# Memory output, norm and router done token tile by token tile, and routing with fp32r parts

## The chip, the cores and the metric

The kernel runs on one NeuronCore of a Trainium2 chip. The metric is the device time of one execution in microseconds. It runs on five engines: TensorE (PE in the profile), VectorE (DVE), ScalarE (ACT), GpSimd (POOL) and SyncE (SP), which here only issues DMAs.

## The reference

One encoder layer over 512 tokens of width 1024 in fp32: a Hyena mixer and a grouped-query attention, an output projection with a residual, a cross attention to 256 memory rows, and a mixture of 16 experts. The part that matters here:

```python
x = x + memory_cross_attn(...)            # ends in  o @ w_o : 512x512 by 512x1024
h = rms_norm(x, norm_moe)
grp_prob = softmax(h @ w_rg + b_rg)       # 4 groups, take the best one
sel = (h @ w_re + b_re)[best group]       # 4 experts in it
w_top, e_loc = top_k(softmax(sel), 2)     # two experts per token
w_top = p_grp * w_top / sum(w_top)
for e in range(16):
    a = silu(h @ w_gate[e]) * (h @ w_up[e])
    y = y + gates[:, e:e+1] * (a @ w_down[e])
x = x + y
```

## The kernel before

The 512 tokens are four tiles of 128. A matmul with fp32 accuracy is made in three fp32r matmuls: each operand is split into a high part (a copy with rounding, by ScalarE) and a low part (a subtraction, by VectorE), and high by high, high by low and low by high are summed in PSUM. The weights ahead of the experts come in 42 pieces of 512 KB through a ring of three slots (`w_raw`, `w_hi`, `w_lo`), loaded by SP in `load_piece`, split by `weight_hi` (L635) and `weight_lo` (L995). Piece 41 is the last quarter of the memory output weights and could be loaded only when piece 38 had been used.

Every engine has one instruction list, written by hand in order, and semaphores tie them. PSUM has eight banks which a list of jobs (`psum_jobs`) hands out in turn; a job opens its bank when the earlier one is freed. There is no planner: the order in each engine's block is the order of the work.

Around the change the order is this. Memory attention runs in eight steps: scores, a maximum, an exponential (ScalarE), a normalisation (VectorE), transposes. Its output is split (`mo`, L640 and L1001). `chunk_jobs` (matmuls at L1698) multiplies by the output weights, piece by piece, each piece over all four token tiles, first the left 512 columns of all tiles and then the right. VectorE adds the residual into `x2` (L1348). Then all of `x2` is transposed (L1650), the transposes are scaled by `norm_moe` and copied to `hT` by both engines (L873, L1407), and only then the router runs for all four tiles, in fp32 (L1643; one fp32 matmul is two records in the trace). ScalarE squares the rows for the norm (L822), VectorE makes `xn` (L1425), and GpSimd stores `xn` to HBM, for the gather.

Routing is a chain of small VectorE instructions (`link` makes each wait for the one before): choice of the group and of two experts as one-hot rows (L1436 to L1462), gate weights (L1466 to L1472), one-hots over 16 experts (L1478, L1481), a count by two fp32 matmuls against a triangular and an all-ones matrix (L1932, L1933), running sums, the place of each token within its expert's block for all 64 columns, then one-hots of places and blocks (L1544 to L1548), an fp32 matmul which turns them into a table of token numbers and gates by block (`records`), and the table of experts (`e_tab`). The table of records is fp32. GpSimd casts a column of it to an int32 index (L532) and gathers 128 rows of `xn` (L536).

An expert block is gathered, transposed (`rows_T`, L1953), split (L899, L1588), multiplied (`gate_up`, `down`, L1958 to L1960), and added into the output by a scatter. Expert weights come in slots of 2 MB, six of them (three kinds, two sets). ScalarE splits them in quarters (L886), VectorE makes the low parts (L1576). The first turn is written out, the rest is a loop over two blocks.

## Time and profile before

| What | us |
|---|---|
| Median of 3 runs | 849.27 (847.8 to 849.71) |
| The profiled execution's own time | 847.16 |
| Its span | 845.3 |
| Output matmuls of the memory attention begin | 473.10 |
| First expert matmul | 544.68 |

| Engine | busy us | share of the span |
|---|---|---|
| PE | 758.9 | 90% |
| PEld | 610.2 | 72% |
| DVE | 595.4 | 70% |
| ACT | 453.8 | 54% |
| POOL | 78.0 | 9% |

PE is the matmul part of TensorE, PEld its weight load, which overlaps PE. Busy time of PE is modelled and counts pipelined matmuls in full. Times in a timeline are from the span's start. The granted clock is the part of 2.4 GHz that TensorE got: 1.00 or 0.50. The span lies inside the execution's own time.

### The profile page before, as it was taken

The numbers are of one execution on the slowest core, as the hardware profiler recorded it, in microseconds if no ns is written. First come the engines' busy times: TensorE is split into PE (matmuls) and PEld (weight loads), VectorE is DVE, ScalarE is ACT, GpSimd is POOL, SyncE is SP. The second block draws the span as 40 slices with busy tenths as digits, with TensorE's granted clock in tenths as the row PEclk, the third lists the DMA queues.
The fourth block names the chain that finished last, engine by engine and source line by source line (L and its number), as shares of the span: only waits on it lengthen the run. The fifth ranks groups of instructions, "written<-read, shape, count | busy, mean of one in ns | idle before, by whom it ended". The sixth has DMA issues, their size and how long they took to land.

```text
span 845.3 us, 10692 instructions
## 1 busy us (share of the span) xinstructions
PE 758.9 (90%) x3632; PEld 610.2 (72%) x3632; DVE 595.4 (70%) x897; ACT 453.8 (54%) x666; POOL 78.0 (9%) x92
## 2 busy tenths in 40 slices
PE   5699999988988899999896992499999999999994
PEld 3564867675777899978774682478888888888883
DVE  5368453994799688633537238578899998999892
ACT  6653323121234766521448151177888878888773
POOL 0000000000000000000000002202232222323101
PEclk9899999999989999979999985599999999999998
DMA  8620303120120200012230059869999999999941
GB/s 286 265 86 16 83 19 98 28 73 1 51 74 26 100 1 2 1 50 74 75 100 1 26 203 344 318 250 359 369 384 366 372 379 382 387 371 373 341 180 20
DMA packets 28542, 146.51 MB, mean 173 GB/s; under 512 B 4792, under 2 KB 6712, under 8 KB 21977
## 3 DMA queue, kind: packets, MB, share of 16 engines
q1 hardware_dynamic: 23320, 135.53, 43.1%
q0 software_dynamic: 5184, 10.50, 4.7%
q8 instruction: 22, 0.36, 0.2%
q14 instruction: 16, 0.12, 0.0%
HBM read 141.81 MB, written 12.58 MB: 183 GB/s over the span
## 4 chain that ended last, share of the span: by engine, by line
PE 76%; DVE 10%; DMA 6%; ACT 5%; issue 2%; SPq 1%; POOL 0%; POOLq 0%; DVEq 0%; ACTq 0%
PE bank L1698 20%; PE bank L1643 18%; PE bank L1958 10%; PE bank L1960 10%; PE bank L1959 10%; PE bank L1650 4%; PE bank L1953 2%; DMA slot<-in_w_down 2%; PE bank L1710 2%; DMA x_in<-in_x 1%; DMA w_raw<-in_w_in 1%; ACT junk L596 1%; ACT w_hi L635 1%; DVE w_lo L995 1%; PE bank L1982 1%
## 5 line engine op out<-in xcount | busy, mean ns | idle before, releaser
L1576 DVE TENSOR_TENSOR e_lo<-slot,e_hi 128x1024 fp32r<-128x1024 f32 x192 | 222.0, 1220 | 14.4 <-ACT e_hi L886 14.3
L886 ACT ACTIVATE e_hi<-slot 128x1024 fp32r<-128x1024 f32 x192 | 188.6, 1061 | 14.3 <-DMA slot<-in_w_down 6.2
L995 DVE TENSOR_TENSOR w_lo<-w_raw,w_hi 128x1024 fp32r<-128x1024 f32 x42 | 50.7, 1223 | 93.0 <-ACT w_hi L635 92.8
L635 ACT ACTIVATE w_hi<-w_raw 128x1024 fp32r<-128x1024 f32 x42 | 43.9, 1062 | 119.1 <-DMA w_raw<-in_w_in 65.9
L1958 PE MATMUL bank<-e_hi,hgT_hi 128*128 128x512 f32 x256 | 102.3, 400 | 3.7 <-DVE hgT_lo L1588 3.7
L1960 PE MATMUL bank<-e_hi,hgT_lo 128*128 128x512 f32 x256 | 100.6, 393 | 0.0
L1959 PE MATMUL bank<-e_lo,hgT_hi 128*128 128x512 f32 x256 | 100.6, 393 | 0.0
L1958 PEld LDWEIGHTS bank<-e_hi,hgT_hi 128*128 128x128 f32 x256 | 48.8, 191 | 13.9 <-DVE hgT_lo L1588 4.3
L1960 PEld LDWEIGHTS bank<-e_hi,hgT_lo 128*128 128x128 f32 x256 | 48.6, 190 | 10.5
L1959 PEld LDWEIGHTS bank<-e_lo,hgT_hi 128*128 128x128 f32 x256 | 48.7, 190 | 9.7
L1958 PE MATMUL bank<-e_hi,gaT_hi 128*128 128x512 f32 x120 | 48.1, 400 | 0.0
L899 ACT ACTIVATE hgT_hi<-bank 128x512 fp32r<-128x512 f32 x32 | 17.3, 595 | 55.3 <-PE bank L1953 55.3
L1960 PE MATMUL bank<-e_hi,gaT_lo 128*128 128x512 f32 x120 | 46.9, 391 | 0.0
L1959 PE MATMUL bank<-e_lo,gaT_hi 128*128 128x512 f32 x120 | 46.8, 390 | 0.0
L1698 PE MATMUL bank<-w_hi,hT_hi 128*128 128x512 f32 (+1 forms) x96 | 35.8, 373 | 4.7 <-DVE w_lo L995 3.2
L1698 PE MATMUL bank<-hT_hi,w_hi 128*128 128x512 f32 x96 | 38.3, 399 | 0.0
L1698 PE MATMUL bank<-hT_lo,w_hi 128*128 128x512 f32 x96 | 37.4, 389 | 0.0
L1698 PE MATMUL bank<-hT_hi,w_lo 128*128 128x512 f32 x96 | 37.4, 389 | 0.0
L1643 PE MATMUL bank<-v_hi,pT_lo 128*128 128x64 f32 x128 | 36.0, 282 | 0.0
L1643 PE MATMUL bank<-v_lo,pT_hi 128*128 128x64 f32 x128 | 35.9, 281 | 0.0
L1643 PE MATMUL bank<-v_hi,pT_hi 128*128 128x64 f32 x128 | 35.9, 281 | 0.0
L1698 PE MATMUL bank<-w_lo,hT_hi 128*128 128x512 f32 (+1 forms) x96 | 35.1, 366 | 0.0
(330 smaller groups left out, 1628.9 us busy)
## 6 DMA issues: line engine op xcount, KB each, us to landing
slot<-in_w_gate SPq DMA_DIRECT2D x16, 2048.0 KB
slot<-in_w_up SPq DMA_DIRECT2D x16, 2048.0 KB, 16.7
slot<-in_w_down SPq DMA_DIRECT2D x16, 2048.0 KB, 15.8
w_raw<-in_w_in SPq DMA_DIRECT2D x18, 512.0 KB, 3.6
w_raw<-in_w_out SPq DMA_DIRECT2D x8, 512.0 KB, 3.7
w_raw<-in_w_k_mem SPq DMA_DIRECT2D x4, 512.0 KB, 6.2
x_in<-in_x SPq DMA_DIRECT2D x4, 512.0 KB, 9.1
w_raw<-in_w_v_mem SPq DMA_DIRECT2D x4, 512.0 KB, 5.4
```

The costliest lines, as they stand in the source:

```text
L635: act.activation(w_hi[m % NSLOT][:], w_raw[m % NSLOT][:], ACT.Copy).then_inc(s_wh, 1)
L886: act.activation(e_hi[buffer(b, j)][:], slot[slot_][:, 1024 * part:1024 * (part + 1)], ACT.Copy).then_inc(s_ehi, 1)
L899: ins = act.activation(hgT_hi[:, 512 * half:512 * (half + 1)], banks[half][:], ACT.Copy)
L995: dve.tensor_tensor(w_lo[slot_][:], w_raw[slot_][:], w_hi[slot_][:].bitcast(F32), ALU.subtract)\
L1576: dve.tensor_tensor(e_lo[slot_][:, at_], slot[slot_][:, at_], e_hi[buffer(b, j)][:].bitcast(F32), ALU.subtract)\
L1643: ins = pe.matmul(dst, l, r, start=(n == 0), stop=(n == len(pairs) - 1))
L1650: ins = pe.transpose(bank(job)[:, n * width:(n + 1) * width], s, ident[:])
L1698: ins = pe.matmul(bank(job)[:, 0:width], left, right, start=(k == 0 and m == 0), stop=(final and m == 2))
L1710: done(pe.matmul(bank(job)[:], a2[:, t * P:(t + 1) * P], w3[way][:, o, :], start=True, stop=True))
L1958: pe.matmul(dst, act_hi, w_hi_, start=first, stop=False)
L1959: pe.matmul(dst, act_hi, w_lo_, start=False, stop=False)
L1960: return pe.matmul(dst, act_lo, w_hi_, start=False, stop=last)
```

## The change

1. The memory output is computed by token tile: both halves of tiles 0 and 1, transposes of tile 0, both halves of tile 2, router of tile 0, transposes of tile 1, and so on (`wom_tile`, `x2T_jobs`, `router_job`). Residual, squares, norm, `xn` and its store follow tile by tile.
2. The last weight piece has a fourth ring slot at 24 KB. It is loaded without waiting for a slot and split inside the memory attention loop.
3. The router multiplies unscaled `x2`, in a high and a low part, with router weights that VectorE scales by `norm_moe` and splits (`wr_split`, 40 columns: high and low). All its matmuls are fp32r. The norm's factor is applied to the logits.
4. The counts are fp32r matmuls that also sum over the tiles. Places and blocks are chosen per token (8 values) and not for all 64 columns. The prefix over experts is a masked sum (`less`) in place of four shift steps.
5. The one-hots of places are eight instructions, each with a semaphore, and the record matmuls follow them one by one. The token number is a record of its own (`rec_i`, int32 at once); gates go through a second matmul later (`rhs_g`, `gates`, `rec_g`).
6. GpSimd's first four gathers read `rec_i` directly. The clearing of the gather buffers goes. The gate records and the expert table are finished after the first rows are split (`tables`).
7. The first block's rows are split by halves with a semaphore for each (`first_rows_hi`, `first_rows_lo`); the matmuls wait for the second half only at the third weight piece.
8. SP loads expert slots 2 and 5 first, slots 0 and 1 after the last tile of the output, 3 and 4 after the last router and all `xn` stores. `xn` moves to 136 KB, so that slot 5 is free.

```diff
-    jobs += [("hT", 2, k) for k in range(KT)]
-    jobs += [("router",), ("count",), ("records",)]
+    jobs += [("wom", 0, 0), ("wom", 1, 0), ("wom", 0, 1), ("wom", 1, 1), ("x2T", 0, 0), ("x2T", 0, 1)]
+    jobs += [("wom", 0, 2), ("wom", 1, 2), ("router", 0), ("x2T", 1, 0), ("x2T", 1, 1)]
+    jobs += [("wom", 0, 3), ("router", 1), ("x2T", 2, 0), ("x2T", 2, 1), ("wom", 1, 3)]
+    jobs += [("router", 2), ("x2T", 3, 0), ("x2T", 3, 1), ("router", 3)]
+    jobs += [("count",), ("records",), ("gates",)]
...
-                sp_.dma_start(slot_view(s), views[s][:, 0]).then_inc(w_ld[s], 16)
+            sp_.dma_start(slot_view(2), views[2][:, 0]).then_inc(w_ld[2], 16)
+            sp_.dma_start(slot_view(5), views[2][:, 1]).then_inc(w_ld[5], 16)
             for i in range(TT):
                 wait_freed(sp_, ("wom", 1, i))
+                if i == TT - 1:
+                    for s in range(2):
+                        sp_.dma_start(slot_view(s), views[s][:, 0]).then_inc(w_ld[s], 16)
                 sp_.dma_start(out[0, i * P:(i + 1) * P, :], x2[:, i, :]).then_inc(s_base, 16)
-            wait_freed(sp_, ("router",))
+            wait_freed(sp_, ("router", TT - 1))
             sp_.wait_ge(s_store, 16 * TT)
             for s in range(3, 5):
                 sp_.dma_start(slot_view(s), views[s - 3][:, 1]).then_inc(w_ld[s], 16)
-            sp_.wait_ge(s_gath[1], 16)
-            sp_.dma_start(slot_view(5), views[2][:, 1]).then_inc(w_ld[5], 16)
             sp_.wait_ge(s_tab, 1)
             nb = sp_.value_load(e_tab[0:1, 31:32], min_val=0, max_val=MAXB - NE) + NE
 
...
 
             def meta(b, q):
 
                 if not isinstance(b, int) or b >= 2:
                     pool.wait_ge(s_oa, b - 1)
...
-                if not isinstance(b, int) or b >= 2:
+                if isinstance(b, int):
+                    index = rec_i[:, b:b + 1]
+                    if b >= 2:
+                        pool.wait_ge(s_t, 2 * b - 2)
+                else:
+                    index = gather_i[:, q, :]
                     pool.wait_ge(s_t, 2 * b - 2)
...
+                if s == 2:
+                    weight_hi(final_piece, 1)
...
+            def x2T_hi(i):
+                for h in range(2):
+                    job = ("x2T", i, h)
+                    wait_filled(act, job)
+                    act.activation(hT_hi[:, 4 * h:4 * h + 4, i * P:(i + 1) * P], bank(job)[:].rearrange("p (k n) -> p k n", k=4),
+                                   ACT.Copy).then_inc(s_hi, 1)
+
+            tile_norm(12, "wom", 10, 0)
+            x2T_hi(0)
+            tile_norm(12, "wom", 10, 1)
+            x2T_hi(1)
...
+            def first_rows_hi():
+                for half, sem_ in ((0, s_first_hi), (1, s_rhi)):
+                    act.wait_ge(s_t, half + 1)
+                    act.activation(hgT_hi[:, 512 * half:512 * (half + 1)], banks[half][:], ACT.Copy).then_inc(sem_, 1)
...
+                if s == 3:
+                    weight_lo(final_piece, 1)
...
+            def x2T_lo(i):
+                for h in range(2):
+                    job = ("x2T", i, h)
+                    dve.wait_ge(s_hi, splits.index(job) + 1)
+                    at_ = (slice(None), slice(4 * h, 4 * h + 4), slice(i * P, (i + 1) * P))
+                    free(dve.tensor_tensor(hT_lo[at_], bank(job)[:].rearrange("p (k n) -> p k n", k=4), hT_hi[at_].bitcast(F32),
+                                           ALU.subtract), job)
+
+            def tile_xn(i):
+                dve.wait_ge(s_rms, 2 + TT + i + 1)
+                link(dve.reciprocal(small[:, 28 + i:29 + i], small[:, 28 + i:29 + i]))
                 dve.scalar_tensor_tensor(xn[:, i, :], x2[:, i, :], small[:, 28 + i:29 + i], g_moe[:], ALU.mult, ALU.mult)\
                     .then_inc(s_xn, 1)
...
+            def tile_logits(i):
+                job, r = ("router", i), small[:, 28 + i:29 + i]
+                wait_filled(dve, job)
+                part_ = rt[:, 2720 + 20 * i:2740 + 20 * i]
+                link(dve.scalar_tensor_tensor(part_, bank(job)[:, 20:40], r, row("b_router"), ALU.mult, ALU.add))
+                free(dve.scalar_tensor_tensor(lg[:, i, :], bank(job)[:, 0:20], r, part_, ALU.mult, ALU.add), job)
...
+            link(dve.tensor_tensor(scaled, wr[:], cols[:, c0:c0 + KT].unsqueeze(2).to_broadcast([P, KT, NG + NE]), ALU.mult))
+            link(dve.tensor_copy(wr_split[:, :, 0:20], scaled))
+            dve.tensor_tensor(wr_split[:, :, 20:40], scaled, wr_split[:, :, 0:20].bitcast(F32), ALU.subtract).then_inc(s_wr, 1)
...
+            dve.wait_ge(ld["g_moe"], 16)
+
+            tile_residual(0, 0)
+            tile_residual(0, 1)
+            tile_residual(1, 0)
+            tile_xn(0)
+            tile_residual(1, 1)
+            x2T_lo(0)
+            tile_residual(2, 0)
+            tile_xn(1)
+            tile_residual(2, 1)
+            x2T_lo(1)
+            tile_residual(3, 0)
+            tile_xn(2)
+            x2T_lo(2)
+            tile_logits(0)
+            tile_logits(1)
+            tile_residual(3, 1)
+            x2T_lo(3)
+            tile_xn(3)
+            tile_logits(2)
+            tile_logits(3)
+            wait_freed(dve, ("router", TT - 1))
...
+            both4 = R3(2816, 4)
+            link(dve.tensor_tensor(both4, oh1, oh2, ALU.add))
+            E12 = onehots[:].rearrange("p (t g e) -> p t g e", t=TT, g=NG)
+            for t in range(TT):
+                dve.tensor_tensor(E12[:, t], ohg[:, t, :].unsqueeze(2).to_broadcast([P, NG, EPG]),
+                                  both4[:, t, :].unsqueeze(1).to_broadcast([P, NG, EPG]), ALU.mult).then_inc(s_oh, 1)
...
+            job = ("count",)
+            wait_filled(dve, job)
+            pos, cnt = bank(job)[:, 0:64], bank(job)[:, 64:80]
+            ov, exc, shift = R(720, 16), R(736, 16), R(752, 16)
+            above(ov, cnt, (128, 256, 384), ALU.is_gt)
+            prefix = rt[:, 1380:1636].rearrange("p (a b) -> p a b", a=NE)
+            link(dve.tensor_tensor(prefix, less[:], ov.unsqueeze(1).to_broadcast([P, NE, NE]), ALU.mult))
+            at_place = R(1100, 128)
+            dve.tensor_tensor(at_place.rearrange("p (r n) -> p r n", r=2), both.rearrange("p (r t) e -> p r (t e)", r=2),
+                              pos.unsqueeze(1).to_broadcast([P, 2, 64]), ALU.mult)
+            link(dve.tensor_reduce(exc, prefix, AX.X, ALU.add))
+            psel = R(1240, 8)
+            dve.tensor_reduce(psel, at_place.rearrange("p (g e) -> p g e", e=NE), AX.X, ALU.add)
+            link(dve.tensor_tensor(shift, exc, x_const, ALU.add))
+            moved = R(1250, 128).rearrange("p (g e) -> p g e", e=NE)
+            hi, xsel, places, blocks = R(780, 8), R(800, 8), R(820, 8), R(840, 8)
+            dve.tensor_tensor(moved, both, shift.unsqueeze(1).to_broadcast([P, 2 * TT, NE]), ALU.mult)
+            link(dve.tensor_scalar(hi, psel, 128.0, None, ALU.is_ge))
+            dve.tensor_reduce(xsel, moved, AX.X, ALU.add)
+            link(dve.scalar_tensor_tensor(hi, psel, 256.0, hi, ALU.is_ge, ALU.add))
+            link(dve.scalar_tensor_tensor(hi, psel, 384.0, hi, ALU.is_ge, ALU.add))
+            dve.scalar_tensor_tensor(places, hi, -128.0, psel, ALU.mult, ALU.add)
+            link(dve.tensor_tensor(R(860, 8), hi, xsel, ALU.add))
+            dve.tensor_tensor(vals, vals, places, ALU.subtract)
+            link(dve.scalar_tensor_tensor(blocks, hi, 0.0, R(860, 8), ALU.is_gt, ALU.mult))
+            link(dve.tensor_tensor(blocks, blocks, chosen, ALU.add))
+            free(dve.tensor_tensor(R(880, 16), exc, ov, ALU.add), job)
+            wait_freed(dve, job)
+            inc = R(880, 16)
+            for g in range(2 * TT):
+                dve.tensor_scalar(place_oh[:, g, :], iota[:], places[:, g:g + 1], None, ALU.is_equal)
+                dve.tensor_scalar(rhs_i[:, g, :], iota[:, 0:MAXB], blocks[:, g:g + 1], vals[:, g:g + 1], ALU.is_equal, ALU.mult)\
+                    .then_inc(s_slot, 1)
+
...
             link(dve.tensor_scalar(R(264, 4), R(204, 4), 1.0, None, ALU.add))
             link(dve.reciprocal(R(264, 4), R(264, 4)))
+            job = ("records",)
+            wait_filled(dve, job)
+            free(dve.tensor_scalar(rec_i[:, 0:MAXB], bank(job)[:, 0:MAXB], col("spare"), None, ALU.add), job)
+            wait_freed(dve, job)
+            dve.sem_inc(s_rec, 1)
...
+            gates, gates_lo = R(268, 8), R(2840, 8)
+            link(dve.tensor_copy(gates_hi[:], gates))
+            link(dve.tensor_tensor(gates_lo, gates, gates_hi[:].bitcast(F32), ALU.subtract))
+            for g in range(2 * TT):
+                dve.tensor_scalar(rhs_g[:, g, 0, :], iota[:, 0:MAXB], blocks[:, g:g + 1], gates_hi[:, g:g + 1].bitcast(F32),
+                                  ALU.is_equal, ALU.mult)
+                dve.tensor_scalar(rhs_g[:, g, 1, :], iota[:, 0:MAXB], blocks[:, g:g + 1], gates_lo[:, g:g + 1],
+                                  ALU.is_equal, ALU.mult).then_inc(s_grhs, 1)
+
+            def tables():
+                job = ("gates",)
+                wait_filled(dve, job)
+                link(dve.tensor_copy(rec_g[:, 0:MAXB], bank(job)[:, 0:MAXB]))
+                free(dve.tensor_tensor(rec_g[:, 0:MAXB], rec_g[:, 0:MAXB], bank(job)[:, MAXB:2 * MAXB], ALU.add), job)
+                wait_freed(dve, job)
+                dve.sem_inc(s_recg, 1)
...
                 act_mul(b)
                 rows_lo(b + 1)
 
-            dve.wait_ge(s_tab, 1)
             turn(0, 0)
...
+            def wom_tile(i, h):
+                job = ("wom", h, i)
+                open_bank(pe, job)
+                n0 = first_piece[f"wom{h}"]
+                for n in (n0, n0 + 1):
+                    pe.wait_ge(s_wl, n + 1)
+                    wh, wl = piece_view(w_hi, n), piece_view(w_lo, n)
+                    for kk in range(2):
+                        k = 2 * (n - n0) + kk
+                        if i == 0 and h == 0:
+                            wait_freed(pe, ("mo", k))
+                        tile_ = slice(i * P, (i + 1) * P)
+                        pe.matmul(bank(job)[:], moT_hi[:, k, tile_], wh[:, kk, :], start=(k == 0), stop=False)
+                        pe.matmul(bank(job)[:], moT_hi[:, k, tile_], wl[:, kk, :], start=False, stop=False)
+                        ins = pe.matmul(bank(job)[:], moT_lo[:, k, tile_], wh[:, kk, :], start=False, stop=(k == MH - 1))
+                done(ins)
...
+            def router_job(i):
+                job = ("router", i)
+                open_bank(pe, job)
+                tile_ = slice(i * P, (i + 1) * P)
+                for h in range(2):
+                    wait_freed(pe, ("x2T", i, h))
+                    for k in range(4 * h, 4 * h + 4):
+                        pe.matmul(bank(job)[:, 0:40], hT_hi[:, k, tile_], wr_split[:, k, :], start=(k == 0), stop=False)
+                        ins = pe.matmul(bank(job)[:, 0:40], hT_lo[:, k, tile_], wr_split[:, k, :], start=False, stop=(k == KT - 1))
+                done(ins)
...
+            x2T_jobs(0)
+            wom_tile(2, 0)
+            wom_tile(2, 1)
+            pe.wait_ge(s_wr, 1)
+            router_job(0)
+            x2T_jobs(1)
+            wom_tile(3, 0)
+            router_job(1)
+            x2T_jobs(2)
+            wom_tile(3, 1)
+            router_job(2)
+            x2T_jobs(3)
+            router_job(3)
...
+            pe.wait_ge(s_oh, TT)
+            pe.matmul(bank(job)[:, 0:64], tri_r[:], onehots[:], start=True, stop=False)
+            for t in range(1, TT):
+                pe.matmul(bank(job)[:, NE * t:64], ones_r[:], onehots[:, 0:64 - NE * t], start=False, stop=(t == TT - 1))
+            done(accumulate(job, bank(job)[:, 64:64 + NE], [(ones_r[:], onehots[:, NE * t:NE * (t + 1)]) for t in range(TT)]))
...
+            for g in range(2 * TT):
+                pe.wait_ge(s_slot, g + 1)
+                ins = pe.matmul(bank(job)[:, 0:MAXB], place_oh[:, g, :], rhs_i[:, g, :], start=(g == 0), stop=(g == 2 * TT - 1))
+            done(ins)
+            job = ("gates",)
+            open_bank(pe, job)
+            pe.wait_ge(s_grhs, 2 * TT)
...
+                else:
+                    pe.wait_ge(s_rlo, b + 1)
...
                 for j in range(8):
                     kind, part = j // 4, j % 4
...
```

## Rows read from the trace of the kernel before

**Rows 1.** the chain of waits, 440 to 600 us; columns: start, us, what

```profile
473.10 21.81 PE bank L1698 x96
...
494.91 3.51 PE bank L1650 x32
...
499.56 11.95 PE bank L1643 x64
...
529.63 3.63 PE bank L1643 x16
...
533.53 0.26 DVE rec_sb L1569
...
535.91 4.20 DMA hg<-xn_dram,gather_i
...
540.24 1.96 PE bank L1953 x8
...
543.34 1.30 DVE hgT_lo L1588 x2
...
544.68 0.80 PE bank L1958
```

**Rows 2.** three stretches: busy time by engine, PE clock, DMA share, GB/s

```profile
300.00:320.00 20.00, 20.00 (x163) 18.79 (x163) 17.00 (x33) 11.77 (x26) 0.00 (x0) 1.00 0.00 1
...
501.80:549.50 47.70, 21.16 (x86) 19.37 (x86) 31.03 (x111) 13.06 (x21) 9.45 (x16) 0.50 0.87 341
...
690.00:710.00 20.00, 20.00 (x95) 16.76 (x94) 18.54 (x19) 16.93 (x22) 5.98 (x6) 1.00 1.00 396
```

**Rows 3.** memory attention loop: ScalarE busy, PE clock, DMA share, GB/s

```profile
451.00:463.50 12.50, 12.49 (x39) 1.00 0.00 1
```

**Rows 4.** timelines of ScalarE and VectorE, the splits of the last weight piece

```profile
482.35 1.06 ACT L635 ACTIVATE w_hi<-w_raw 128x1024 fp32r<-128x1024 f32 x1 [8.61 <-DMA w_raw<-in_w_o_mem]
...
483.44 1.23 DVE L995 TENSOR_TENSOR w_lo<-w_raw,w_hi 128x1024 fp32r<-128x1024 f32 x1 [8.98 <-ACT w_hi L635]
```

**Rows 5.** timeline of TensorE, attention, first and last of twelve matmuls

```profile
298.85 0.28 PE L1643 MATMUL bank<-v_hi,pT_hi 128*128 128x64 f32 x1
...
300.08 0.28 PE L1643 MATMUL bank<-v_hi,pT_lo 128*128 128x64 f32 x1
```

**Rows 6.** timelines of ScalarE and VectorE, operations on halves and tiles

```profile
473.14 0.60 ACT L640 ACTIVATE moT_hi<-bank 128x512 fp32r<-128x512 f32 x1 [1.12 <-PE bank L1643]
...
501.25 1.04 ACT L822 ACTIVATE junk<-x 128x1024 f32<-128x1024 f32 x1
...
473.77 0.69 DVE L1001 SCALAR_TENSOR_TENSOR moT_lo<-bank,moT_hi 128x512 fp32r<-128x512 f32 x1 [1.03 <-ACT moT_hi L640]
...
484.59 2.48 DVE L1348 TENSOR_TENSOR x<-x,bank 128x512 f32<-128x512 f32 x4
...
505.68 4.87 DVE L1425 SCALAR_TENSOR_TENSOR xn<-x,small,g_moe 128x1024 f32<-128x1024 f32 x4
```

**Rows 7.** timeline of VectorE, routing and the first expert pieces

```profile
512.24 0.17 DVE L1436 TENSOR_REDUCE rt<-rt 128x4 f32<-128x16 f32 x1
...
516.24 0.18 DVE L1445 TENSOR_TENSOR rt<-rt 128x16 f32<-128x16 f32 x1
...
518.48 0.22 DVE L1481 TENSOR_TENSOR rt<-rt 128x64 f32<-128x64 f32 x1
...
533.69 4.63 DVE L1576 TENSOR_TENSOR e_lo<-slot,e_hi 128x1024 fp32r<-128x1024 f32 x4
```

**Rows 8.** timeline of GpSimd, the index cast

```profile
533.92 1.03 POOL L532 CAST gather_i<-rec_sb 128x1 int32<-128x1 f32 x1 [20.69 <-DVE rec_sb L1569]
```

**Rows 9.** DMA issues in three short windows; last column us to landing

```profile
xn_dram<-xn POOLq DMA_DIRECT2D x1, 512.0 KB, 15.0
...
g_moe<-in_g_moe SPq DMA_DIRECT2D x1, 512.0 KB, 3.8
...
slot<-in_w_up SPq DMA_DIRECT2D x1, 2048.0 KB, 12.3
```

313 lines of the change are left out of this document (135 added, 178 removed).

## The prediction

> **What bounds the kernel now.** I read the chain of waits first, then the granted clock by stretch, then the timelines of the four engines between 440 and 560 us, last the expert stage. The reader is to see three things.
>
> First, the expert stage (from 544.68 us to the end) is a convoy of TensorE. In [rows 2] the stretch 690 to 710 has PE busy for all 20 us at clock 1.00, with the DMA engines at 1.00 too. TensorE does not wait there, so whatever makes the stage begin earlier moves the whole stage, with its tail, by that much; its weight loads are released by TensorE's own progress and move with it. Second, everything between the memory output and the first expert matmul is one chain [rows 1]: 96 output matmuls from 473.10, 32 transposes, 64 router matmul records from 499.56, small VectorE instructions, the record matmuls at 529.63, the gather at 535.91, transposes at 540.24, the low halves at 543.34, and the expert matmuls at 544.68. That is 71.6 us with one engine at a time. Third, TensorE runs at half clock (granted 0.50, 1.2 of 2.4 GHz) from 501.8 to 549.5 [rows 2]: it fell behind the dense output matmuls, under transposes and 20-column matmuls.
>
> I cost the change against this chain, in four steps, in the time of the profiled execution (span 845.3, its own time 847.16), and carry the difference to the median of 849.27, which lies 2.1 above it.
>
> **Step A, the last weight piece (+2.4).** Piece 41 gets a slot of its own, loads right behind piece 40, and its split moves from 482.35 (ScalarE 1.06) and 483.44 (VectorE 1.23), where both engines idled, into the memory attention loop [rows 4]. There ScalarE is busy 12.49 of 12.5 us [rows 3], so its 1.06 less 0.1 of overlap goes straight onto the path: +1.0. VectorE must then wait for that split before its own 1.23, with the loop's next maximum and normalisation queued behind; the two engines hand to each other each step, so I count another 0.9. The load of piece 40 is waited for by ScalarE and now has piece 41 0.4 us behind it: +0.5. Bounds: 0.5 (all absorbed) to 4. The output matmuls begin at 475.5 instead of 473.1. Call that t0.
>
> **Step B, output, residual, norm, router by tile (-4.6).** Before: 473.1 to 512.24, when VectorE starts routing [rows 7]: 39.1 us. After, TensorE's own work: 96 output matmuls 21.8 (21.81 for 96 [rows 1], 0.227 each, unchanged); transposes 8 per tile at 0.11, 0.9 per tile; router 16 fp32r matmuls of 40 columns per tile. No row has this shape. The nearest are the attention's 64-column fp32r matmuls, eleven steps from 298.85 to 300.08, 0.112 each at full clock [rows 5]; the bounds are half of that and, at half clock, 0.22 (the record matmuls: 3.63 for 16 [rows 1]). I take 0.112, 1.8 per tile. TensorE order: all eight output groups, three tiles of transposes (2.6) and two routers (3.6) end at t0+28.1. Then the third router and last transposes run to t0+30.8, while VectorE adds the last residual (0.62 [rows 6]) and ScalarE squares and roots it (1.04 for the square [rows 6], 1.5 in all by my estimate), so ScalarE is free at t0+30.4. High halves 0.60 and low halves 0.69 [rows 6] of the two half tiles overlap: all ready at t0+32.3, the last router matmuls end at t0+33.4. VectorE still has the last norm product (1.2 [rows 6]) and four small logit instructions: routing begins at t0+34.6 = 510.1. The residuals of the earlier tiles, their squares, halves and xn products (18 us of VectorE work) lie under 28 us of matmuls. VectorE starts them only when g_moe has landed, 3.8 after its issue [rows 9], at about t0+6; the first tile is needed by TensorE at t0+10.9, so this is covered with 3.5 to spare. Should the clock already be at half for the final router, +1.5.
>
> **Step C, routing (-6.8).** Before: 512.24 to 533.79 [rows 1, 7], 21.5 us. After, by VectorE's pace of one dependent small instruction per 0.2 us. Selection as before, 4.2 [rows 7], then one small sum and four products: one-hots at +4.9 instead of +6.5, because the gate arithmetic (six instructions) and half of the one-hots move behind. Count on TensorE: 8 fp32r matmuls in place of 4 records, at half clock 0.22 each: 2.2 with the hand-over. Places chosen per token: some 21 instructions, a good half of them dependent, two over 256 elements which I put at 0.45 (between 0.2 for 16 columns and 0.62 for 512 [rows 6]): 4.1. Eight place one-hots with their columns, at 0.25 a pair: 2.0, and TensorE's eight record matmuls follow behind each, in place of 3.63 after the last. Then VectorE has six gate instructions in its queue ahead of the record read: 1.25, which covers the last record matmul. The record read with its cast to int32: 0.3. Sum 4.9+2.2+4.1+2.0+1.25+0.3 = 14.75. Bounds: 12 (overlap inside the independent pairs) to 18. Records ready at 524.9.
>
> **Step D, gather to first expert matmul (-3.1).** Before: 533.79 to 544.68, 10.9 us. The cast on GpSimd (1.03 [rows 8]) and its own semaphore go: the gather is issued 0.5 after the record instead of 2.1. It lands after 4.2 [rows 1]; the first four transposes take 1.0 (1.96 for eight [rows 1]); the high and low half 0.60 and 0.69: 7.2. But VectorE, which in the old kernel split the first four expert pieces (4.63 [rows 7]) while the gather flew, now first has two gate products, a rounding, a subtraction and 16 small gate columns: 2.4, then 4.63, then the first low half 0.69: 7.8 with hand-over. VectorE ends last; 7.8 stands. Behind it the table work (2.7) sits before expert pieces 4 and 5; their first use is 24 matmuls later, 7.5 at half clock and 5.5 at full, and they are ready 4.5 after the start. So the tables cost nothing; without this cover they would cost up to 2.7.
>
> **The moved loads.** SP issues expert pieces 2 and 5 at about 477.5, behind g_moe, and 0 and 1 only at t0+28.8 = 504.3. A pair of 2 MB loads landed in 12.3 [rows 9]; ScalarE has them by 517, and VectorE wants them at 527.3. Pieces 3 and 4 still wait for the last router and for all xn stores. The last xn store is issued near 509.4; before, such a store took 15.0 to land [rows 9], with some 10 MB in flight; here 5 MB are. Even 15.0 gives 524.4, just under the records at 524.9, for which the gather waits as well. Pieces 3 and 4 then land by 537 and are wanted near 541. The cleared gather buffers (two memsets on GpSimd) were under the routing: nothing.
>
> **One rule weighed.** [Rows 7] and [rows 1] show the gather issued at 535.91 while VectorE ran two-input subtractions, and nothing slow in it. The Trainium skill, "SBUF — State Buffer", section "Who interferes with whom", says that one-source VectorE instructions (copy, cast, tensor_scalar) in a two-port mode keep GpSimd out of the shared port, so that it cannot write the descriptors of its own DMA. Here the gather is written just while VectorE runs the gate columns, which are such instructions. No run so far shows it; it is the fourth rival below.
>
> **Sum.** +2.4 - 4.6 - 6.8 - 3.1 = -12.1. Expert matmuls begin at 532.6. 847.16 - 12.1 = 835.1 for a profiled execution, 849.27 - 12.1 = 837.2 for the median.
>
> **The rivals.**
> 1. *The clock falls at the first router block* (t0+17.3) and stays at 1.2 GHz. Then 15.3 us of TensorE work (two output tiles with their transposes and routers) doubles: +15, 852, slower. It decides from 12.1 us of extra. For it: the clock fell just there in the old order, 7 us behind the last dense matmul [rows 2]. Against: dense 2.7 to 5.5 us groups stand between the small ones, and the attention, with 64-column matmuls, transposes and a few wide ones mixed, holds 1.00 [rows 2]. Chance 0.06. A partial form, from the third router on: +3.6, 840.8, chance 0.12.
> 2. *The last xn store holds the gather* and pieces 3 and 4: at a landing of 20 instead of at most 15, +4.5, 841.7. For it: 15.0 already stands within 0.5 of the path. Against: half the bytes in flight. 0.07.
> 3. *The tiles don't overlap*, because VectorE is held for g_moe: landing like a store (13 and more) it would delay the first residual to 490 and TensorE by 5: 842. Against: 3.8 in the same company before. 0.05.
> 4. *GpSimd's descriptors wait for VectorE's gate columns*: the gather is written 2.4 later, of which 0.6 is slack: +1.8, 839. 0.10.
>
> **How the numbers follow.** Forecast 0.60, with steps A to D at their own bounds 833 to 841. The range 831.5 to 843.5 takes in rivals 2 to 4 and the partial clock, and leaves out the full clock case and unforeseen waits. This kernel's measurement tells about 0.2% (1.7 us) from no change. Faster: 0.92; within: 0.02; slower 0.06.
>
> **What would show it.** A: output matmuls begin near 475.5, ScalarE's split of the last piece inside the loop. B: granted clock 1.00 up to about 505, routing begins near 510. C: records near 525, VectorE without gaps except one of about 0.6 before the count. D: gather issued within 0.5 of the record, first expert matmul near 532.6, its first low half last. Expert stage: TensorE without a gap as before, and as long. Wrong if the clock is at 0.50 by 495, if the first expert matmul comes after 542, or if the stage, once begun, runs longer than its 300 us.

## The result, and the profile after

The changed kernel takes 839.15 us (median of 4 runs, 834.61 to 841.46) against 849.49 in the same session: ratio 0.989 [0.985, 0.993]. Forecast: 837.2, range 831.5 to 843.5, faster with 0.92. Its profiled execution takes 837.83 us (span 835.8) where 835.1 was forecast. The time was right to 2 us, partly by luck: an error in one step took off what an error in another had added (see the sum below).

The chain of waits after; it answers to [rows 1]:

```profile
474.36 0.23 PE bank L2025
...
502.17 0.24 PE bank L2027
...
506.10 0.26 PE bank L2042
...
510.05 0.18 DVE rt L1531
...
525.14 0.25 DVE rec_i L1626
...
529.66 4.54 DVE e_lo L1665 x4
...
534.19 0.61 DVE hgT_lo L1677
...
534.85 0.80 PE bank L2099
```

The first output matmul is at 474.36 (473.10 before), routing begins at 510.05 (512.24), the record is ready at 525.38 (533.79), the first expert matmul starts at 534.85 (544.68). The gather no longer stands in this chain: VectorE's low halves of the expert weights end last. The stage behind it is as long as before (300.95 us to the end, 300.62 before), so in these two profiles it moved as a whole. The windows, as in [rows 2] (columns: busy us by engine, TensorE clock, DMA share, GB/s):

```profile
501.80:506.30 4.50, 3.43 (x29) 3.15 (x28) 1.93 (x4) 3.03 (x6) 0.00 (x0) 1.00 0.49 132
506.30:547.00 40.70, 23.92 (x90) 20.33 (x90) 34.32 (x130) 15.21 (x19) 4.26 (x8) 0.58 0.67 261
690.00:710.00 20.00, 20.00 (x95) 16.74 (x95) 18.54 (x20) 16.94 (x22) 5.16 (x7) 1.00 1.01 384
```

The clock is at its higher level until the last tile's router and falls inside it. ScalarE, VectorE and TensorE in the memory loop, where [rows 4] had nothing (timelines: start, us, instruction, idle before it and its releaser):

```profile
459.04 1.06 ACT L662 ACTIVATE w_hi_last<-w_raw_last 128x1024 fp32r<-128x1024 f32 x1
...
460.13 1.22 DVE L1040 TENSOR_TENSOR w_lo_last<-w_raw_last,w_hi_last 128x1024 fp32r<-128x1024 f32 x1 [0.74 <-ACT w_hi_last L662]
...
462.14 0.66 PE L1746 MATMUL bank<-ident,pr 128*128 128x128 f32 x4 [1.97 <-DVE pr L1434]
...
467.26 7.11 PE L1739 MATMUL bank<-mpT,mv 128*128 128x512 f32 x16 [1.10 <-ACT mpT L886]
```

VectorE waits 0.74 for ScalarE's split, then spends 1.22 on its own, and TensorE idles 1.97 ahead of its fifth group of transposes. In the kernel before it had no gap there and one of 1.05 a step later:

```profile
460.69 0.66 PE L1650 MATMUL bank<-ident,pr 128*128 128x128 f32 x4
...
462.40 0.66 PE L1650 MATMUL bank<-ident,pr 128*128 128x128 f32 x4 [1.05 <-DVE pr L1389]
```

In the changed kernel that later gap is 0.87, so the two together cost 1.79 more. (The value matmuls, L1739 with `mpT` and `mv`, multiply the transposed probabilities by the memory's values; there are sixteen of 512 columns, and they end the loop.) VectorE in the routing; it answers to [rows 7]:

```profile
514.47 0.43 DVE L1564 TENSOR_TENSOR onehots<-rt 128x16 fp32r<-128x16 f32 x4
...
517.01 0.17 DVE L1580 TENSOR_SCALAR rt<-bank 128x16 f32<-128x16 f32 x1 [0.78 <-PE bank L1739]
...
521.12 0.29 DVE L1614 TENSOR_SCALAR place_oh<-iota,rt 128x128 fp32r<-128x128 f32 x1
521.33 0.29 DVE L1615 TENSOR_SCALAR rhs_i<-iota,rt 128x24 fp32r<-128x24 f32 x1
...
524.30 0.18 DVE L1619 TENSOR_REDUCE rt<-rt 128x4 f32<-128x16 f32 x1
...
525.14 0.24 DVE L1626 TENSOR_SCALAR rec_i<-bank,cols 128x24 int32<-128x24 f32 x1
...
526.33 0.30 DVE L1635 TENSOR_SCALAR rhs_g<-iota,rt,gates_hi 128x24 fp32r<-128x24 f32 x1
...
526.93 0.52 DVE L1637 TENSOR_SCALAR rhs_g<-iota,rt 128x24 fp32r<-128x24 f32 x1
...
529.55 4.64 DVE L1665 TENSOR_TENSOR e_lo<-slot,e_hi 128x1024 fp32r<-128x1024 f32 x4
```

The eight pairs take 3.2 us (0.2 for each instruction, 24 columns wide or 128). GpSimd's gather, where the cast of [rows 8] is gone, and the landings of the last xn store and of the gather, answering to [rows 9] (last column: us from issue):

```profile
526.38 1.09 POOL L562 DMA_INDIRECT hg<-xn_dram,rec_i  x1 [17.62 <-DVEq L1628]
```

```profile
xn_dram<-xn POOLq DMA_DIRECT2D x1, 512.0 KB, 9.6
...
hg<-xn_dram,rec_i POOLq DMA_INDIRECT x1, 5.1
```

### The profile page after: what moved, and what is told of

It reads as the page before. It is cut to its first block, busy times and chain, and to the rows that moved or that the text cites. A ratio compares the mean times of both kernels' runs of the same rounds, so it can differ in the third digit from the quotient of the medians.

```text
span 835.8 us, 10729 instructions
## 1 busy us (share of the span) xinstructions
PE 762.1 (91%) x3636; PEld 611.9 (73%) x3636; DVE 603.5 (72%) x937; ACT 456.4 (55%) x670; POOL 73.4 (9%) x86
## 4 chain that ended last, share of the span: by engine, by line
PE 76%; DVE 10%; DMA 6%; ACT 5%; issue 2%; SPq 1%; POOL 0%; DVEq 0%; POOLq 0%; ACTq 0%
PE bank L1794 18%; PE bank L1739 16%; PE bank L2099 10%; PE bank L2101 10%; PE bank L2100 10%; PE bank L1746 4%; DMA slot<-in_w_down 2%; PE bank L1806 2%; PE bank L2094 2%; DMA x_in<-in_x 1%; PE bank L2027 1%; PE bank L2026 1%; PE bank L2025 1%; DMA w_raw<-in_w_in 1%; ACT junk L623 1%
## 5 line engine op out<-in xcount | busy, mean ns | idle before, releaser
L1665 DVE TENSOR_TENSOR e_lo<-slot,e_hi 128x1024 fp32r<-128x1024 f32 x192 | 221.8, 1220 | 11.2 <-ACT e_hi L926 10.9
L662 ACT ACTIVATE w_hi<-w_raw 128x1024 fp32r<-128x1024 f32 x41 | 42.9, 1063 | 111.7 <-DMA w_raw<-in_w_in 66.6
L1739 PE MATMUL bank<-v_hi,pT_lo 128*128 128x64 f32 x128 | 35.5, 277 | 0.0
L1739 PE MATMUL bank<-v_lo,pT_hi 128*128 128x64 f32 x128 | 35.5, 277 | 0.0
L1739 PE MATMUL bank<-v_hi,pT_hi 128*128 128x64 f32 x128 | 35.5, 277 | 0.0
L1794 PE MATMUL bank<-w_lo,hT_hi 128*128 128x512 f32 (+1 forms) x96 | 34.5, 360 | 0.0
L1794 PE MATMUL bank<-w_hi,hT_lo 128*128 128x512 f32 (+1 forms) x96 | 34.5, 359 | 0.0
```

The lines of the kernel that those rows point to most:

```text
L662: act.activation(w_hi[ring(m)][:], w_raw[ring(m)][:], ACT.Copy).then_inc(s_wh, 1)
L1665: dve.tensor_tensor(e_lo[slot_][:, at_], slot[slot_][:, at_], e_hi[buffer(b, j)][:].bitcast(F32), ALU.subtract)\
L1739: ins = pe.matmul(dst, l, r, start=(n == 0), stop=(n == len(pairs) - 1))
L1794: ins = pe.matmul(bank(job)[:, 0:width], left, right, start=(k == 0 and m == 0), stop=(final and m == 2))
```

## The experiments

Twelve runs in three sessions. The kernel before had medians of 846.53, 846.75 and 848.11 us in them; the ratios are against it. They are the ratios on record and not quotients of two medians, from which they differ by up to 0.003 (for e8 0.9841 and 0.987). All were profiled, and their profiles put side by side, in us:

```
                          first loop      ->       ->       -> first   ->
                          transpose ->    routing  record   expert     end
                          output matmul   begins   ready    matmul
before                    18.50           39.70    21.54    10.90      300.62
split in loop alone       23.27           38.69    21.54    11.22      302.48
changed, first profile    20.27           36.25    15.33     9.47      300.95
changed, e0               23.86           35.12    15.32    10.26      298.88
changed, e12              22.77           35.98    15.30     9.45      301.87
e3 no interleave          23.30           36.61    15.30     9.46      300.28
e4 wide gates             23.25           35.32    15.30     9.92      302.18
e9 gap filled             20.26           35.78    15.30     9.49      300.72
e1 split behind loop      18.48           35.02    15.29    10.39      299.02
e8 the same again         20.18           35.65    15.33     9.62      301.83
e5 e1 + wide, gates late  20.19           35.62    14.49    10.64      299.43
e6 e5 + loads held        18.50           34.99    14.50     8.18      304.02
e10 e1 + routing filled   20.17           34.98    15.24    10.67      300.18
e11 e5 + routing filled   20.18           35.02    14.30    11.59      299.88
```

(The output matmul is taken where the timeline has its first record, 0.56 ahead of the chain's start for it.) Profiles are single executions. Columns two to four repeat within about 1 us for the same code. In column two the last tile's router begins 32.3 after the first output matmul in every version but e3 and the two old ones; what follows depends on where in it the clock falls (not at all in e1, e6, e10 and e11, with 35.0). The first column does not repeat, and the clock is why (below). So it is with the last: 301.8 to 304.0 in e4, e6, e7, e8 and e12, where the granted clock is 0.83 to 0.92 both over 10 to 20 and over 280 to 290 us behind the first expert matmul; 300.3 and 300.7 in e3 and e9, with the first of these dips alone; 298.9 to 300.95 in the others, with neither.

**e0_after**, the changed kernel itself, as the yardstick of the first session.

> The changed kernel again, as the reference of this chip and for its spread. My theory of the change: 10 us faster than before (about 839), with the same landmarks in the trace: output matmuls begin 1.3 to 2.5 us later than in the kernel before if both reach the memory attention together, routing takes 15.3, the way from the records to the first expert matmul 9.5. Rival for its spread (834.6 to 841.5 in four runs): stretches of half clock ahead of the changed part, in the attention, fall differently from run to run; then the time from the first transposes of the memory attention to the end agrees within 1 us between two profiles, while the time up to them differs by several.

Measured: 840.07 us (10 runs, 834.81 to 841.22), 0.9907 [0.9874, 0.9939]. This profile has what the first one did not: the clock falls in the memory loop. TensorE's timeline, and a window over it:

```profile
464.26 0.66 PE L1746 MATMUL bank<-ident,pr 128*128 128x128 f32 x4 [2.37 <-DVE pr L1434]
...
469.84 9.85 PE L1739 MATMUL bank<-mpT,mv 128*128 128x512 f32 x16 [1.10 <-ACT mpT L886]
```

```profile
466.00:470.00 4.00, 2.90 (x13) 2.12 (x13) 1.40 (x6) 2.44 (x7) 0.00 (x0) 0.50 0.00 0
```

The sixteen value matmuls take 9.85 instead of 7.11: the granted clock is 0.50 (1.2 GHz) from about 465.1 to 475.4 and 1.00 from there on. The gather ends last here: its flight is on the chain with 6.62 us, and the first expert matmul waits for it and not for VectorE's expert pieces:

```profile
530.56 6.62 DMA hg<-xn_dram,rec_i
```

The rival of the expectation, that only what lies ahead of the memory attention differs, fails: from the loop's first transposes to the end the changed kernel takes 382.3 (first profile), 383.4 (e0) and 385.4 us (e12), where it asked for agreement within 1.

**e1_split_in_gap and e8_split_in_gap_again**: step A undone in part. The last piece keeps its own slot and early load, but both halves are split just behind the loop:

```diff
-                if s == 2:
-                    weight_hi(final_piece, 1)
+            weight_hi(final_piece, 1)
             for h in range(MH):
                 split_hi(("mo", h), moT_hi[:, h, :])
...
-                if s == 3:
-                    weight_lo(final_piece, 1)
+            weight_lo(final_piece, 1)
             for h in range(MH):
                 split_lo(...)
```

> The split of the last weight piece moves from inside the memory attention loop to the gap behind it, where both engines wait for the mo matmuls. Theory (step A): in the loop it lies on the path, so from the first transposes of the loop to the first mo matmul 1.8 us go (13.7 becomes 12.0, as in the kernel before), and the kernel is 1.8 us faster than the changed one. Rival: the loop is held by TensorE and the other waits, and the split costs nothing there: 0, the 1.8 come from elsewhere. Second rival: behind the loop the split delays the halves of mo and the first output group: 0 or slower.

> The kernel of the second run once more (split behind the loop, all else changed), for its spread and a second profile, and as the reference of the next two. Theory: the clock stays at 1.00 from the loop through the mo matmuls, 18.5 us to the first output matmul, median near 834, 5 to 6 us faster than the changed kernel. Rival (luck): the fall is chance and comes here too: 20 to 23 us, median 838 to 840.

Measured: 833.97 (0.9857 [0.9812, 0.9902]) and 835.53 (0.9841 [0.9814, 0.9867]). Beside e0, in the same session, e1 is 6.1 us lower by the medians (831.4 to 838.1 against 834.8 to 841.2). By the ratios, which compare across sessions, the two are 0.003 to 0.007 below the changed kernel's 0.9889 to 0.9907, or 3 to 6 us. With e5 and e6 they are the fastest versions of this study. TensorE's timeline of e1:

```profile
459.75 0.66 PE L1744 MATMUL bank<-ident,pr 128*128 128x128 f32 x4 [1.05 <-DVE pr L1433]
...
463.34 7.11 PE L1737 MATMUL bank<-mpT,mv 128*128 128x512 f32 x16 [1.09 <-ACT mpT L886]
```

No gap of 2 us, loop and value matmuls as long as before. The two splits (1.05 and 1.23 here) lie where both engines wait for the value matmuls. In the profile of e8 the same code lost the clock all the same, but later, under the value matmuls, and for 3 to 4 us, which cost 1.7:

```profile
466.14 8.80 PE L1737 MATMUL bank<-mpT,mv 128*128 128x512 f32 x16 [1.10 <-ACT mpT L886]
```

**e7_before_split_in_loop**: step A alone. The kernel before, with the slot of its own for piece 41 and the splits at s == 2 and s == 3 of the loop, and nothing else of the change:

```diff
                     mem_exp(s + MAHEAD)
+                if s == 2:
+                    weight_hi(final_piece, 1)
...
                     mem_max(s + MAHEAD)
+                if s == 3:
+                    weight_lo(final_piece, 1)
```

> The kernel before with step A alone: own slot for the last weight piece, its split inside the memory attention loop; all else as before. Theory: the split holds both engines, TensorE stands idle for 2 us in the loop, and in most executions the clock then falls to 0.50, so that the last transposes and the mo matmuls run at half. From the loop's first transposes to the first output matmul 20.3 us where the clock holds and 23.3 to 23.9 where it falls, against 18.5 before; the kernel 2 to 5 us slower than before, and with a wider spread. Rival 1: the clock fell in three profiles because of what came earlier (the start of the loop at half clock), not because of the gap; then this one keeps 1.00 in the loop and is 1.8 slower. Rival 2: the delay belongs to the other changes; then within 0.2% of before.

Measured: 852.53 us (848.07 to 854.11) where before has 846.75: 1.005 [1.0025, 1.0074], so 4.2 us slower, 2.1 to 6.3 by the interval (5.8 by the medians). TensorE's timeline shows gap and fall again:

```profile
463.21 0.71 PE L1663 MATMUL bank<-ident,pr 128*128 128x128 f32 x4 [1.97 <-DVE pr L1401]
...
468.78 9.65 PE L1656 MATMUL bank<-mpT,mv 128*128 128x512 f32 x16 [1.10 <-ACT mpT L870]
```

**e9_gap_filled and e12_after_again**: is the gap what lowers the clock? Ten identity transposes on TensorE ahead of the wait at s == 4, in the bank that the real ones then overwrite, beside the changed kernel once more:

```diff
+            def fill(job, n):
+                open_bank(pe, job)
+                for _ in range(n):
+                    pe.transpose(bank(job)[:, 0:P], ident[:], ident[:])
...
+                if s == 4:
+                    fill(("MPT", s), 10)
                 pe.wait_ge(s_mnorm, s + 1)
```

> The changed kernel with ten more 128x128 transposes of the identity on TensorE in the memory loop, ahead of its wait for the fifth probability tile (the 2 us gap that the in-loop split of the last weight piece opens); they write the bank that the real transposes overwrite, and end before these may start (10 x 0.165 = 1.65 us of a gap of 1.97 to 2.37). Theory one: the gap is why the granted clock falls to 0.50 in the loop (4 of 5 profiles with the in-loop split), so with it filled the clock is 1.00 through the loop and the mo matmuls (x16) take 7.1 us and not 9.6 to 9.9; from the first loop transpose to the first output matmul 20.3 us as where the clock held, and the time falls by 2 to 3 us against the changed kernel (about 837.5 where it is 840). Theory two: the clock falls for other reasons (the loop's small matmuls altogether); then mo stays at 9.6 to 9.9 and the time is that of the changed kernel, or up to 1.5 us above it if ten transposes at the half clock (3.3 us) outlast the gap.

> The changed kernel once more, beside the three filled ones. By both theories 838 to 841 with the spread seen before (834.8 to 841.2); if the in-loop gap is what lowers the clock, this profile shows the mo matmuls at 9.6 to 9.9 us more likely than at 7.1 (four of five so far).

Measured: 838.9 (834.0 to 840.05), 0.9888 [0.9846, 0.993], beside 839.33 (837.44 to 843.82), 0.9897 [0.9857, 0.9937]. TensorE's timeline of e9:

```profile
461.32 1.26 PE L1745 MATMUL bank<-ident 128*128 128x128 f32 x10
463.45 0.66 PE L1751 MATMUL bank<-ident,pr 128*128 128x128 f32 x4 [0.87 <-DVE pr L1434]
...
468.56 7.11 PE L1739 MATMUL bank<-mpT,mv 128*128 128x512 f32 x16 [1.10 <-ACT mpT L886]
```

The profile is as the gap theory has it: the clock holds, the idle time is 0.87. It is one profile, and the first of the changed kernel held the clock without a filler. The times don't part the two (0.4 us, with intervals of 3.5 to either side), where the theory wanted 2 to 3 us. So: the gap's 1.8 us is shown; that it draws the clock down has five profiles of six with an unfilled gap for it (e0, e3, e4, e7, e12, not the first), and no time. The rival that the expectation of e7 names, that what came earlier decides, is not excluded. In all fourteen profiles the clock was at half some way ahead of the loop and was back 1 to 7 us before the loop's first transposes. By that alone they don't part: it was back 1.1 to 1.2 before in e3, e4 and e7, which fell 0.4 to 0.5 behind the gap, and 1.3 before in e9, which held. No run varied it.

**e3_no_interleave**: step B undone in its order, with the rest of the change kept. All output tiles, then all transposes, then all routers:

```diff
+            for i in range(TT):
+                wom_tile(i, 0)
+                wom_tile(i, 1)
+            for i in range(TT):
+                x2T_jobs(i)
+            pe.wait_ge(s_wr, 1)
+            for i in range(TT):
+                router_job(i)
```

(in place of the mixed order; ScalarE's and VectorE's calls follow it.)

> The new operations in the old order: all eight output groups, then all transposes, then all four routers; residual, norm and xn still by tile where the matmuls allow. Theory (step B): what the mixed order gains is that small matmuls stand between dense groups and the clock stays at 1.00 until the last tile. Then here the clock falls under the routers, some 7 us behind the last dense group, and routing begins 1 to 4 us later after the output matmuls begin than the changed kernel's 35.7. Rival (overlap): the gain is that norm, halves and residual lie under matmuls; then the last tile's work is exposed in one piece and it is 3 to 6 us later at an unchanged clock. Second rival: the order gives nothing, it is the merged scaling and norm that gained; then routing begins within 0.7 of 35.7.

Measured: 841.03, 0.9932 [0.9898, 0.9965], against 0.9907 for e0. These two runs are of one session, and their times are not told apart. From output to routing 36.61 us against 35.12 to 36.25 for the changed kernel. Here too the clock falls under the last routers, in a window that TensorE fills:

```profile
508.00:512.00 4.00, 4.00 (x21) 4.00 (x20) 2.25 (x7) 0.00 (x0) 0.53 (x1) 0.50 1.03 382
```

By these single profiles the order is worth 0.4 to 1.5 of step B's 3.5 us, where the changed kernel's own three differ by 1.1. The rest goes with what e3 keeps: residuals and norm by tile, and the router in fp32r parts (64 matmuls of 40 columns, where there were 64 records in 11.95 at half clock). Those two were not tried apart.

**e4_wide_gates**: the 16 gate columns as three wide products:

```diff
-            for g in range(2 * TT):
-                dve.tensor_scalar(rhs_g[:, g, 0, :], iota[:, 0:MAXB], ..., ALU.is_equal, ALU.mult)
-                dve.tensor_scalar(rhs_g[:, g, 1, :], ...)
+            dve.tensor_tensor(block_oh, iota..., blocks..., ALU.is_equal)
+            dve.tensor_tensor(rhs_g[:, :, 0, :], block_oh, gates_hi..., ALU.mult)
+            dve.tensor_tensor(rhs_g[:, :, 1, :], block_oh, gates_lo..., ALU.mult)
```

> The 16 small gate columns (3.3 us of VectorE between the records and the first expert pieces) become one block one-hot and two wide products (1.0). Theory (step D): VectorE ends last, but the gather is close behind: issued 1.0 after the records, landing 5.1, then 1.0 for four transposes, 0.6 and 0.7 for the halves, 8.5 in all, against 9.5 now. So the first expert matmul comes 1.0 us sooner after the records, and the kernel is 1.0 faster than the changed one. Rival 1: VectorE alone sets it: 2.3 sooner. Rival 2: the gate matmuls or the gather set it already: 0.

Measured: 838.28, 0.9893 [0.9845, 0.9941], not told apart from e0. VectorE's timeline:

```profile
527.41 0.35 DVE L1639 TENSOR_TENSOR rhs_g<-rt 128x192 fp32r<-128x192 f32 x1
527.68 4.62 DVE L1667 TENSOR_TENSOR e_lo<-slot,e_hi 128x1024 fp32r<-128x1024 f32 x4
535.07 0.69 DVE L1679 TENSOR_TENSOR hgT_lo<-bank,hgT_hi 128x512 fp32r<-128x512 f32 x1 [2.77 <-ACT hgT_hi L939]
```

VectorE starts on the expert pieces 1.8 after the record instead of 4.2 and then waits 2.77 for the gathered rows: its gain turned into a wait for the gather, which took 6.3 here.

**e5_all**: e1, the block one-hots of the records wide as well, and all gate work behind the first expert pieces:

```diff
-            for g in range(2 * TT):
-                dve.tensor_scalar(place_oh[:, g, :], ...)
-                dve.tensor_scalar(rhs_i[:, g, :], ...)
+            link(dve.tensor_tensor(block_oh, iota..., blocks..., ALU.is_equal))
+            link(dve.tensor_tensor(rhs_i[:], block_oh, vals..., ALU.mult))
+            for g in range(2 * TT):
+                dve.tensor_scalar(place_oh[:, g, :], ...).then_inc(s_slot, 1)
...
-                    lo_parts(b, q, 4, 8)
+                    lo_parts(b, q, 4, 7)
+                    gate_columns()
+                    lo_parts(b, q, 7, 8)
                     lo_parts(1, 1, 0, 4)
+                    gate_records()
```

> Split behind the loop; block one-hots and columns as wide products for the records and the gates; gate columns, gate matmuls and gate records only after the first block's expert pieces, beside its matmuls. Theory: records 0.9 sooner (16 small instructions become 8 and two wide ones); after them VectorE takes 4.6 for the expert pieces and the gather ends last, issued 1.0 after the records and landing 4.2 to 6.9: 8 to 10 us to the first expert matmul, so about 0 to 1 gained there. In all 1 to 2 us faster than the kernel with the split behind the loop. Rival 1: VectorE set the way to the first expert matmul: 9.5 becomes 6.5, 3 to 4 faster. Rival 2: late gates delay the second gather round and the first turn's product: 0 or slower.

Measured: 835.26, 0.9851 [0.9824, 0.9878]: no better than e8. The record comes 0.84 earlier (VectorE's timeline):

```profile
521.20 0.36 DVE L1612 TENSOR_TENSOR rt<-iota,rt 128x192 f32<-128x192 f32 x1
521.60 0.36 DVE L1614 TENSOR_TENSOR rhs_i<-rt 128x192 fp32r<-128x192 f32 x1
521.99 1.66 DVE L1616 TENSOR_SCALAR place_oh<-iota,rt 128x128 fp32r<-128x128 f32 x8
```

But the gather, issued earlier, flew 7.0 us on the chain, and the first expert matmul came 10.64 after the record.

**e6_loads_behind_gather**: e5 with slots 3 and 4 loaded only when the first gather has landed:

```diff
             sp_.wait_ge(s_store, 16 * TT)
+            sp_.wait_ge(s_gath[0], 16)
             for s in range(3, 5):
```

> The same with the loads of expert slots 3 and 4 held until the first gather has landed. Theory (the gather is slowed by 4 MB of weights in flight): the gather lands 2.9 to 3.5 after its issue in place of 4.2 to 6.9, the first expert matmul comes 7 to 7.5 after the records, 1.5 to 2.5 us better. But slots 3 and 4 land 12.3 after the gather, some 2 us before their first use by ScalarE. Rival 1: the landing is the gather's own latency (stores to HBM, 128 descriptors) and doesn't change: 0. Rival 2: the weights of the second block come late and TensorE waits in the second turn: slower by 2 to 4.

Measured: 834.43, 0.9844 [0.982, 0.9868]: e5's time. The chain shows the gather's flight at 4.54 us, beside no weight load, against e5's 7.0 (2.9 to 3.5 were expected):

```profile
519.80 4.54 DMA hg<-xn_dram,rec_i
```

The first expert matmul comes 8.18 after the record, 2.5 sooner than in e5, and the stage behind it is 4.6 longer. Windows of e6 and of e5, both from 20 to 30 us behind the first expert matmul:

```profile
546.98:556.98 10.00, 10.00 (x42) 8.18 (x41) 7.51 (x7) 6.74 (x7) 0.00 (x0) 0.91 0.74 277
```

```profile
555.27:565.27 10.00, 10.00 (x50) 8.42 (x49) 7.70 (x7) 6.59 (x8) 0.00 (x0) 1.00 0.78 281
```

TensorE is busy for all of both; e6 has the lower clock. Over the first three such stretches e6 has 0.76, 0.92 and 0.91 where e5 has 0.84, 1.00 and 1.00, which makes 2.5 us, and the transposes of the third block's rows are 2.4 later. The other 2.2 are lost behind the last rows' transposes, where e6 takes 42.9 to the end and e5 40.6; but e4, e8 and e12, whose loads are not held, take 42.3 to 42.6 there, so that part is not the loads' doing. Whether the held loads bring about the first is open: one profile, and a time that shows neither gain nor loss.

**e10_routing_filled and e11_all_filled**: e1 and e5 with idle TensorE fed in the routing by the same fill():

```diff
+            fill(("router", 3), 5)
             router_job(3)
             job = ("count",)
-            open_bank(pe, job)
+            fill(job, 16)
...
             job = ("records",)
-            open_bank(pe, job)
+            fill(job, 14)
```

(e10 also 14 ahead of the gates; e11 24 ahead of the gathered rows.)

> The split of the last weight piece behind the memory loop (e1), and idle TensorE fed with transposes of the identity in the routing: 5 ahead of the last tile's router matmuls (1.07 us idle), 16 ahead of the count (5.6 idle), 14 ahead of the records (4.9 idle), 14 ahead of the gates (5.0 idle); at half clock 16 last 5.3 us, so that they end about when the real work may begin. Theory one (activity holds the clock): the granted clock is above 0.50 in much of 508 to 536, the records matmuls take 1.5 instead of 3.08, the row transposes 1.0 instead of 1.9, the first expert matmuls run at the full clock; first expert matmul 1.5 to 3 us earlier and the expert stage up to 2 shorter: 831 to 832 where e1 is 835. Theory two (fillers of this size do not lift it, since they fill half of the time and the router and records matmuls stay small): the clock stays 0.50 and the time is e1's, up to 1.5 us above where a filler outlasts its gap.

> The version with the split behind the loop, the wide block one-hots and the gate columns behind the gather's issue (e5), with transposes of the identity on TensorE: 5 ahead of the last router, 16 ahead of the count, 14 ahead of the records and 24 ahead of the gathered rows' transposes (8.5 us idle). Theory one: the clock is 1.00 by the first expert matmul, which comes 1 us earlier, and the first two blocks lose less: about 832 where e5 is 835.3. Theory two: the clock stays at 0.50 until the expert matmuls have run for some us as in all profiles so far; 835, or up to 1.5 above.

Measured: 837.12, 0.986 [0.9816, 0.9903], and 837.25, 0.9876 [0.9835, 0.9917]: e1's time at best. Window and timeline of e10:

```profile
508.00:512.00 4.00, 1.64 (x16) 1.40 (x13) 3.45 (x23) 0.22 (x1) 0.53 (x1) 1.00 0.98 418
```

```profile
507.67 1.97 PE L1743 MATMUL bank<-ident 128*128 128x128 f32 x16
...
515.23 3.25 PE L1743 MATMUL bank<-ident 128*128 128x128 f32 x14
```

The clock holds through the last router and the first filler. Through the router it held in e1 and e6 as well, without fillers, and from output to routing these have the same 35.0; so that is not shown to be the fillers' doing. In e10 it is then at 0.50 for the second filler, comes up to 0.79 over 528 to 532 (the eight gate matmuls take 1.07 instead of 1.87), and is at 0.50 again for the gathered rows. At the first expert matmul it is at 0.50 in e10 and 0.53 in e11. The routing, VectorE's, gains 0.1. With these fillers TensorE still idles 1.7 to 4.1 us at all waits but one, and they don't bring the higher clock to where TensorE is the bound again.

## Why the prediction was right, and which steps were off

**Step A, predicted +2.4, is the step that failed.** Its mechanism (both splits on the path of a saturated hand-over, 1.0 + 0.9) is what the first profile shows, +1.77 inside the loop. The load's +0.5 lies ahead of the loop, where this column doesn't look: piece 40 was waited for 3.88 to 4.06 in the thirteen profiles that load piece 41 behind it and 3.65 in the kernel before, so 0.2 to 0.4 of it came. The sum left a term out: the 2 us gap on TensorE, after which the clock was at half in five of six profiles, the value matmuls at 9.6 to 9.9 (8.9 in e12) for 7.1. Then the step costs 4.3 to 5.4 by the first column of the table. That is against 18.50, the kernel before's only profile; the loop without the splits took 20.2 in four of its seven profiles, and the means of six with (22.8) and seven without (19.5) differ by 3.3. That fits the times: alone, the step costs 4.2 by the ratio, 2.1 to 6.3 by its interval (e7). [Rows 3] showed ScalarE busy for 12.49 of 12.5 us and TensorE at clock 1.00; I priced the first and took the second for granted.

**Step B, predicted -4.6, measured -3.45** (39.14 to 35.69, chain to chain). The work up to the last output matmul took 28.05 us where 28.1 was worked out. The error is the last router: from the third of its sixteen matmuls on they come 0.21 apart, not 0.11, so it falls to half clock at 506.3, and the +1.5 that the text held ready for that fell due, as 1.1. Where the clock held through it (e1, e6) routing began 34.4 to 34.5 after t0, for 34.6 forecast. By e3 only 0.4 to 1.5 of the step is the tile order, which I had not separated from the cheaper router.

**Step C, predicted -6.8, measured -6.21.** One-hots 4.87 (4.9), count to places 2.1 (2.2), places 4.11 (4.1), the four gate instructions and the record 1.1 (six and 1.55). The eight pairs took 3.18 for 2.0: I gave 0.25 to a pair, and each of its instructions costs 0.2.

**Step D, predicted -3.1, measured -1.43.** VectorE did end last, as forecast, but with 4.0 for gate work where I had 2.4, for the same reason: 16 columns of 0.2. The gather was issued 1.0 after the record (0.5) and landed 5.1 after issue (4.2). In e0, e1, e4, e5, e6, e8, e10 and e11 the gather is on the chain. In the first profile it is close behind: the rows' transposes begin at 531.59 and ScalarE's high half of the first four follows without a wait for anything else:

```profile
532.72 0.60 ACT L939 ACTIVATE hgT_hi<-bank 128x512 fp32r<-128x512 f32 x1 [15.18 <-PE bank L2094]
```

So from 533.3 on only VectorE was missing, which was free at 534.09. A shorter gate work could have gained 0.8 there and nothing where the gather is last, and e4 shows no gain in time. The tables ran from 535.3 to 537.9 behind the expert matmuls, and cost nothing.

**The sum.** +1.77 - 3.45 - 6.21 - 1.43 = -9.32, with the 0.51 by which this execution reached the loop earlier -9.83; forecast -12.1. The error of +2.2 at the first expert matmul is A -1.1, B +1.1, C +0.6, D +1.7, so what A had too much hid about what B had too little: that is the luck in the figure, and half of A's part is the 0.51, which no term forecast. In the median, A is dearer: without the in-loop split (e1, e8) the kernel stands at 0.9857 and 0.9841, 12 and 13 us below before (12.6 and 11.2 by the medians), where B to D alone had 14.5 in the forecast.

**The rivals.** The clock did not fall at the first router block; it fell one tile later than even the partial form had it, and, in a place no rival named, in the loop ahead. The last xn store landed 9.6 after its issue at 508.23, 7.5 before the record. g_moe landed in 4.0, and the first residual began at 480.88, t0 + 6.5 where I had t0 + 6. The fourth: the gather's issue on GpSimd took 1.09 us beside VectorE's gate columns, 1.10 before beside subtractions with two inputs, so GpSimd was not held up. By the Trainium skill, "SBUF — State Buffer", section "Who interferes with whom", it could have been; the trace does not agree here. What shows is the other side: one column beside each of the two gathers' issue took 0.52 and 0.43 instead of 0.30. Where the gate columns had gone and VectorE ran the subtractions instead (e5, e6, e11), the two issues took 1.32 and 1.90 for 1.09 and 1.02; since the kernel before had 1.10 beside the same subtractions, the cause is open.

## What to carry to other kernels

Before work is moved into a loop in which two engines hand to each other without slack, look where a gap of equal length already stands: the same two splits cost 2 to 6 us in the loop, and behind it nothing that the timeline shows. Count small VectorE instructions one by one by the issue interval that the profile shows (0.2 us), not by width, and make one wide product of a column loop. When the bound of a hand-over is cut, measure the second arrival first; here the gather, which ended 0.8 us ahead of VectorE in the first profile and last in eight others, took what the shorter gate work gave. And compare profiles only at equal clock: the changed kernel's own differ by 3.6 us in the loop and 3.0 in the expert stage.
